# End of a feed-forward part: the last two up pairs first, then three down blocks by token chunk, with the weight ring turned one slot per layer

## The chip, the core and the metric

The kernel runs on one core of one Trainium2 chip. The metric is the device time of one execution in microseconds (us). Five engines work side by side, each through its own list in order: PE (TensorE, matmuls; PEld is its weight load), DVE (VectorE), ACT (ScalarE), POOL (GpSimd, which here only starts transfers) and SP (SyncE, which starts the weight transfers). They meet in semaphores.

## The reference

A trunk of two layers over 256 tokens of width 1024. Each layer has a mixer half and a feed-forward half, both between RMSNorms, with shift, scale and gate vectors computed from `c`:

```python
for l in range(DEPTH):                       # DEPTH = 2
    mod = c_act @ ada_w[l] + ada_b[l]
    sh_m, sc_m, g_m, sh_f, sc_f, g_f = jnp.split(mod, 6, axis=-1)
    h = modulate(rmsnorm(x, mix_pre_g[l]), sh_m, sc_m)
    y = mixer_sublayer(h, ...)
    x = x + g_m[:, None, :] * rmsnorm(y, mix_post_g[l])
    h = modulate(rmsnorm(x, ffn_pre_g[l]), sh_f, sc_f)
    up = causal_dwconv(h @ w_up, conv_w, conv_b)      # width 3, D_FF = 2816
    u, g = up[..., :D_FF], up[..., D_FF:]
    y = (jax.nn.gelu(g) * u) @ w_down
    x = x + g_f[:, None, :] * rmsnorm(y, ffn_post_g[l])
```

## The kernel before

**Split products.** Every f32 weight block and every activation is split into a high part and a low part, and a product is three matmuls (`mm3`, L1597). A weight block of 128 x 2048 goes through four stations: SP loads it into a slot of `raw`; ACT writes `w_hi` (L548, L925); DVE writes `w_lo` as the difference (L1039, L1541); PE multiplies. `raw`, `w_hi` and `w_lo` are rings of 3 slots (`RING`). SP may load a slot again when DVE has split its block (`lo_ready`), ACT may write `w_hi` when PE has used the block (`blk_used`). `SLOT[j]` says which slot block j of a layer takes: blocks 0 to 39 (`NM` = 40) are the mixer's, 40 to 72 (`NB` = 73) the feed-forward part's.

**Feed-forward part.** 22 tiles of the hidden width are worked in 11 pairs (`PAIRS`). Pair i has a gate block g(i), a value block u(i) (both up projections, 48 matmuls of 256 columns each) and a down block d(i). PE runs g(i), u(i), then d(i-1), which is 12 matmuls of 512 columns for token chunk 0 and 12 for chunk 1 (`down_proj`, L2034); the sums stay in banks 0 to 3. After g(i) and after u(i) ACT and DVE take the convolution out of the bank (`conv`, L902 and L1514), and then split the blocks that come next; `hidden` (L1532), `hidden_hi` (L917) and `hidden_lo` (L1536) make the input of d(i). The last pair ends with d(9) and d(10), each chunk 0 and then chunk 1. `gate_rows` (L1626) turns the gate vector into a row, in two halves, before g(10) and after u(10).

**Tile sums.** The shift, scale and gate vectors of the next parts are computed on DVE: tile by tile of `ada_w`, 128 x 1024 each, multiplied by `c` and summed (`ada_sum`, L1032, `ffn_sum`, L1557). POOL loads the tiles into two buffers of `adw` (L500): the load of tile n waits for the sum of tile n-2. In layer 0 the feed-forward part has 24 sums, most of them two to a pair; the last of them complete shift and scale of layer 1. Layer 1 has none from pair 3 on.

**End of a part.** `half_end` on DVE (L1132) begins with shift and scale (L1081, L1084), which need all sums. Then come `gated` for the two halves of chunk 0 (L1117, each after ACT's square of it, L616), `residual` of chunk 0 (L1129), the split of the next layer's block 0, `gated` of the first half of chunk 1, and `inverse_rms` (L1074, L1076), whose `diag` PE waits for with `to_features` (L1618). Then PE runs four filler matmuls (`keep_going`, L1632), the first product of the next layer, and `to_features` of chunk 1. At the end of layer 1 only `gated`, `residual` and the output transfers are left.

Of the kernel before, what the change touches and what calls it, by code (L numbers as in the profile page):

```python
# [21 lines left out]
P = 128  # L22
# [10 lines left out]
RING = 3  # L33
# [86 lines left out]
def trunk_kernel(nc, A, consts, out):  # L120
# [70 lines left out]
    assert SLOT[-RING:] == SLOT[:RING] == list(range(RING))  # L191
# [3 lines left out]
    def previous(j):  # L195

        before = [b for b in range(j) if SLOT[b] == SLOT[j]]
        return before[-1] if before else max(b for b in range(NB) if SLOT[b] == SLOT[j]) - NB

    ctx = ExitStack()  # L200
    with ctx:
# [74 lines left out]
        raw_in = [sig(f"raw_in{s}", 16 * USES[s]) for s in range(RING)]  # L276
# [89 lines left out]
        def slot_in(j):  # L366

            return raw_in[SLOT[j]]
# [9 lines left out]
        def block_shape(t, j):  # L378

            _, k, cols = mixer_blocks[j]  # L380
            return t[:, SLOT[j], 0:k * cols].rearrange("p (k n) -> p k n", k=k)

        def kv_parts(t, j, packed):


            v = t[:, SLOT[j], :].bitcast(F32) if packed == "read" else t[:, SLOT[j], :]
# [6 lines left out]
        def uq_parts(t, j, packed):  # L393


            v = t[:, SLOT[j], 0:QK * 4 * DQK]
# [26 lines left out]
        def _(sp):  # L423
# [4 lines left out]
            for n in range(ADA0):  # L428
# [5 lines left out]
                if n == 7:  # L434
                    j, (src, k, cols) = 0, mixer_blocks[0]
                    sp.dma_start(block_shape(raw, j), src(0)).then_inc(slot_in(j).s, 16)
            for l in range(L):
                for j, (src, k, cols) in enumerate(mixer_blocks):
# [3 lines left out]
                    sp.wait_ge(lo_ready.s, lo_ready.at(l, RING + previous(j) + 1))  # L442
# [4 lines left out]
                    sp.dma_start(block_shape(raw, j), src(l)).then_inc(slot_in(j).s, 16)  # L447
# [13 lines left out]
                def load(j_wait, slot, kind, src):  # L461
                    sp.wait_ge(lo_ready.s, lo_ready.at(l, j_wait))
                    sp.sem_inc(sp_tick, 1)
                    sp.dma_start(ffn_shape(raw, slot, kind), src).then_inc(raw_in[slot].s, 16)


                load(NM + 1, SLOT[NM], "up", up(l, FF, BW))
                load(NM + 2, SLOT[NM + 1], "up", up(l, 0, BW))
                with sp.Fori(1, PAIRS) as i:
                    load(3 * i + NM, SLOT[NM + 2], "up", up(l, i * BW + FF, BW))  # L470
                    load(3 * i + NM + 1, SLOT[NM + 3], "up", up(l, i * BW, BW))
                    down = A["ffn_w_down"][bass.ds(l, 1)].rearrange("a (k p) n -> p (a k) n", p=P)
                    load(3 * i + NM + 2, SLOT[NM + 4], "down", down[:, bass.ds(2 * i - 2, 2), :])
                down = A["ffn_w_down"][bass.ds(l, 1)].rearrange("a (k p) n -> p (a k) n", p=P)
                load(NB, SLOT[NB - 1], "down", down[:, 2 * PAIRS - 2:2 * PAIRS, :])
# [39 lines left out]
        def _(act):  # L515
# [27 lines left out]

            def split_hi(l, j, dst, src):

                act.wait_ge(slot_in(j).s, slot_in(j).at(l, 16 * (NTH[j] + 1)))
                act.wait_ge(blk_used.s, blk_used.at(l, RING + previous(j) + 1))
                A_(dst, src, ACT.Copy).then_inc(hi_ready.s, 1)  # L548

            def split_block(l, j):  # L550
                if j == J[("c", 2)]:

                    r = block_shape(raw, j)
                    d = w_hi[:, SLOT[j], :].rearrange("p (k n) -> p k n", k=DK)
                    act.wait_ge(slot_in(j).s, slot_in(j).at(l, 16 * (NTH[j] + 1)))
                    act.wait_ge(blk_used.s, blk_used.at(l, RING + previous(j) + 1))
# [3 lines left out]
                elif j == J[("ukv", 0)]:  # L560
                    act.wait_ge(slot_in(j).s, slot_in(j).at(l, 16 * (NTH[j] + 1)))
                    act.wait_ge(blk_used.s, blk_used.at(l, RING + previous(j) + 1))
                    for d, r in zip(kv_parts(w_hi, j, True), kv_parts(raw, j, False)):
                        a = A_(d, r, ACT.Copy)
                    a.then_inc(hi_ready.s, 1)
                elif j in (J[("uq", 0)], J[("uq", 1)]):
                    act.wait_ge(slot_in(j).s, slot_in(j).at(l, 16 * (NTH[j] + 1)))
                    act.wait_ge(blk_used.s, blk_used.at(l, RING + previous(j) + 1))
                    for d, r in zip(uq_parts(w_hi, j, True), uq_parts(raw, j, False)):
                        a = A_(d, r, ACT.Copy)  # L570
                    a.then_inc(hi_ready.s, 1)
                elif j < NM:
                    split_hi(l, j, block_shape(w_hi, j), block_shape(raw, j))
                else:
                    split_hi(l, j, w_hi[:, SLOT[j], :], raw[:, SLOT[j], :])
# [113 lines left out]
            for l in range(L):  # L689
# [210 lines left out]
                def conv(n, part, i, first=False):  # L900

                    product_done(act, l, NM + part if first else i * 3 + (NM - 1 + part))  # L902
# [12 lines left out]
                def hidden_hi(i, half=0):  # L915
                    act.wait_ge(f_t.s, f_t.at(l, i + 1))
                    A_(flat2(oa_hi, half), flat2(tmp, 0), ACT.Copy).then_inc(f_hi.s, 1)  # L917

                def ffn_split(i, part):

                    slot = SLOT[NM + 2 + part]
                    j = i * 3 + (NM + 2 + part)
                    act.wait_ge(raw_in[slot].s, raw_in[slot].at(l, i * 16 + 16 * (NTH[NM + 2 + part] + 1)))
# [9 lines left out]
                with act.Fori(1, PAIRS - 1) as i:  # L933
# [8 lines left out]
                i = PAIRS - 1  # L942
                gate_rows(l, 1, 0, 6)
# [4 lines left out]
                hidden_hi(i, 1)  # L948
# [10 lines left out]
        def _(dve):  # L959
# [81 lines left out]
            def split_block(l, j):  # L1041
                if j == J[("c", 2)]:
                    r = block_shape(raw, j)
                    h = w_hi[:, SLOT[j], :].bitcast(F32).rearrange("p (k n) -> p k n", k=DK)
                    d = w_lo[:, SLOT[j], :].rearrange("p (k n) -> p k n", k=DK)
# [1073 lines left out]
```

## Time and profile before

| | us |
|---|---|
| median of 3 runs | 997.36 (997.17 to 997.51) |
| profiled execution, its own time | 995.64 |
| its span in the trace | 994.0 |
| granted PE clock, mean | 0.991 |

The span is what the trace covers; some 1.6 us of the execution's time lie around it. Durations below come from this one execution. The "idle before" of an instruction names what ended the idle time. Matmul records overlap, since they are pipelined: the step from one to the next is what a matmul costs PE.

### The profile page before, as it was taken

How to read it: one execution, taken by the hardware profiler on the slowest of the kernel's cores; microseconds unless marked ns; L12 is line 12 of the kernel's file. 1: busy time of each engine (PE TensorE's matmuls, PEld its weight loads, DVE VectorE, ACT ScalarE, POOL GpSimd, SP SyncE). 2: the span in 40 equal slices, each digit the busy share in tenths (PEclk: the TensorE clock that was granted, in tenths of full speed). 3: DMA queues.
4: the chain of work that ended last, by engine and by line, in shares of the span. 5: the costliest groups of instructions: out<-in, count | busy, mean ns of one | idle time of the engine just before them, and what ended most of it. 6: DMA issues, size and time to landing. Idle time of an engine off the chain costs nothing.

```text
span 994.0 us, 17872 instructions
## 1 busy us (share of the span) xinstructions
PE 959.8 (97%) x6976; PEld 897.2 (90%) x6976; DVE 717.7 (72%) x958; ACT 526.3 (53%) x701; POOL 43.6 (4%) x85
## 2 busy tenths in 40 slices
PE   6899999999998999999989999999999999999997
PEld 6799989999987999999969999899999799999996
DVE  4689766676667888787776966677667689676675
ACT  4346855455446654554574475643445656554544
POOL 0000000000000100000000000000000000000000
PEclk9799999999999999999999999999999999999999
DMA  9985755556572787777636864556646557555541
GB/s 356 374 258 177 247 161 165 192 191 213 173 265 73 270 301 247 241 246 239 241 115 192 276 211 156 157 175 224 228 137 225 185 193 273 187 183 181 180 156 43
DMA packets 134138, 206.35 MB, mean 208 GB/s; under 512 B 6336, under 2 KB 104384, under 8 KB 133952
## 3 DMA queue, kind: packets, MB, share of 16 engines
q1 hardware_dynamic: 122416, 162.07, 49.9%
q0 software_dynamic: 11520, 41.95, 11.5%
q10 hardware_dynamic: 144, 1.51, 0.4%
q8 instruction: 42, 0.69, 0.3%
q14 instruction: 16, 0.13, 0.0%
HBM read 204.46 MB, written 1.05 MB: 207 GB/s over the span
## 4 chain that ended last, share of the span: by engine, by line
PE 88%; DVE 4%; ACT 3%; DMA 2%; SPq 1%; issue 1%; DVEq 0%; ACTq 0%
PE banks L1602 78%; DMA raw<-in_w_in 2%; PE banks L1618 1%; DVE w_lo L1039 1%; SPq L449 1%; PE banks L1888 1%; PE banks L1891 1%; PE banks L1626 1%; PE banks L1732 1%; PE banks L1714 1%; DMA raw<-in_ada_rows 1%; ACT h L597 1%; ACT w_hi L548 1%; DVE x L1129 1%; PE banks L1662 1%
## 5 line engine op out<-in xcount | busy, mean ns | idle before, releaser
L1602 PE MATMUL banks<-h_lo,w_hi 128*128 128x256 f32 x1504 | 430.5, 286 | 3.4 <-DVE h_lo L1100 3.0
L1602 PE MATMUL banks<-h_hi,w_lo 128*128 128x256 f32 x1504 | 425.5, 283 | 0.0
L1602 PE MATMUL banks<-h_hi,w_hi 128*128 128x256 f32 x1504 | 425.5, 283 | 0.0
L1602 PEld LDWEIGHTS banks<-h_lo,w_hi 128*128 128x128 f32 x1504 | 288.4, 192 | 7.1 <-DVE h_lo L1100 3.8
L1602 PEld LDWEIGHTS banks<-h_hi,w_lo 128*128 128x128 f32 x1504 | 288.5, 192 | 2.2 <-issue 1.4
L1602 PEld LDWEIGHTS banks<-h_hi,w_hi 128*128 128x128 f32 x1504 | 288.4, 192 | 0.0
L1039 DVE TENSOR_TENSOR w_lo<-raw,w_hi 128x2048 fp32r<-128x2048 f32 x82 | 187.2, 2290 | 71.0 <-ACT w_hi L548 70.8
L548 ACT ACTIVATE w_hi<-raw 128x2048 fp32r<-128x2048 f32 x82 | 156.0, 1911 | 120.1 <-PE banks L1602 99.1
L1541 DVE TENSOR_TENSOR w_lo<-raw,w_hi 128x2048 fp32r<-128x2048 f32 x56 | 128.0, 2286 | 22.6 <-ACT w_hi L925 22.6
L925 ACT ACTIVATE w_hi<-raw 128x2048 fp32r<-128x2048 f32 x56 | 107.2, 1914 | 41.8 <-PE banks L1602 41.8
L1518 DVE SCALAR_TENSOR_TENSOR EF<-banks,par,EF 128x254 f32<-128x254 f32 (+1 forms) x176 | 76.7, 477 | 49.9 <-ACT EF L906 44.5
L906 ACT ACTIVATE EF<-banks,par 128x256 f32<-128x256 f32 x88 | 45.1, 563 | 104.0 <-PE banks L1602 104.0
L1602 PE MATMUL banks<-w_hi,oa_lo 128*128 128x512 f32 x208 | 81.3, 391 | 0.0
L1602 PE MATMUL banks<-w_lo,oa_hi 128*128 128x512 f32 x208 | 81.2, 390 | 0.0
L1602 PE MATMUL banks<-w_hi,oa_hi 128*128 128x512 f32 x208 | 80.9, 389 | 0.0
L500 POOL DMA_DIRECT2D adw<-in_ada_rows x80 | 42.4, 531 | 792.5 <-DVE adw L1032 600.5
L1032 DVE SCALAR_TENSOR_TENSOR adw<-adw,cbc 128x1024 f32<-128x1024 f32 x58 | 70.4, 1221 | 5.7 <-DMA adw<-in_ada_rows 4.4
L836 ACT ACTIVATE lat<-banks 128x512 f32<-128x512 f32 x24 | 14.2, 590 | 74.6 <-PE banks L1602 74.6
L1602 PEld LDWEIGHTS banks<-w_hi,oa_hi 128*128 128x128 f32 x208 | 39.1, 188 | 8.2
L1602 PEld LDWEIGHTS banks<-w_hi,oa_lo 128*128 128x128 f32 x208 | 39.1, 188 | 7.6
L1602 PEld LDWEIGHTS banks<-w_lo,oa_hi 128*128 128x128 f32 x208 | 39.1, 188 | 7.4
L1602 PE MATMUL banks<-oa_lo,w_hi 128*128 128x256 f32 x128 | 37.2, 290 | 1.6 <-DVE EF L1467 1.6
(280 smaller groups left out, 1238.9 us busy)
## 6 DMA issues: line engine op xcount, KB each, us to landing
raw<-in_w_in SPq DMA_DIRECT2D x52, 1024.0 KB, 6.1
raw<-in_ffn_w_up SPq DMA_DIRECT2D x44, 1024.0 KB, 5.1
adw<-in_ada_rows POOLq DMA_DIRECT2D x80, 512.0 KB, 4.7
raw<-in_ffn_w_down SPq DMA_DIRECT2D x22, 1024.0 KB, 4.9
raw<-in_w_out SPq DMA_DIRECT2D x8, 1024.0 KB, 7.7
raw<-in_ret_wo SPq DMA_DIRECT2D x4, 1024.0 KB, 5.0
raw<-in_lru_wo SPq DMA_DIRECT2D x4, 1024.0 KB, 7.2
raw<-in_mla_wo SPq DMA_DIRECT2D x4, 1024.0 KB, 6.9
```

Source lines behind the costliest of these rows:

```text
L449: sp.dma_start(pos_i, A["positions"][0, :].partition_broadcast(P)).then_inc(pos_in, 16)
L500: pool.dma_start(adw[:, slot, :], ada_v[:, bass.ds(n + ADA0, 1), :].rearrange("p a d -> p (a d)")).then_inc(adw_in[slot], 16)
L548: A_(dst, src, ACT.Copy).then_inc(hi_ready.s, 1)
L597: a = A_(h32[:, k, cs], PS[:, ACT_BANK[c][half], P * i:P * i + P], ACT.Identity, scale=hscale[:, k:k + 1], bias=mod[:, k:k + 1])
L836: A_(flat2(lat, m % 2), PS[:, gate_bank(m), :], ACT.Tanh, scale=0.5).then_inc(mg_th.s, 1)
L906: a = A_(EF[:, 2 * part + b, :], PS[:, 4 + part, T * b:T * b + T], ACT.Identity, scale=par[:, l, bass.ds(i * 2 + col["tap2"] + NFF * (1 - ...
L925: A_(w_hi[:, slot, :], raw[:, slot, :], ACT.Copy).then_inc(hi_ready.s, 1)
L1032: V.scalar_tensor_tensor(adw[:, n % 2, :], adw[:, n % 2, :], 1.0, cbc[:], ALU.mult, ALU.mult, accum_out=mraw[:, n % NT:n % NT + 1]).then_i ...
L1039: V.tensor_tensor(dst, whole, hi, ALU.subtract).then_inc(lo_ready.s, 1)
L1518: v = V.scalar_tensor_tensor(EF[:, 2 * part + b, d:T], PS[:, 4 + part, T * b:T * b + T - d], par[:, l, bass.ds(i * 2 + col[f"tap{tap}"] + ...
L1541: V.tensor_tensor(w_lo[:, slot, :], raw[:, slot, :], w_hi[:, slot, :].bitcast(F32), ALU.subtract).then_inc(lo_ready.s, 1)
L1602: ins = MM(ps, lhs, rhs, start=first and n == 0, stop=last and n == 2)
```

## The change

It has four parts.

1. PE's order at the end of each feed-forward part: g(9), u(9), first half of `gate_rows`, g(10), u(10), second half, then d(8), d(9) and d(10) as d(8) chunk 0, d(9) chunk 0, d(8) chunk 1, d(10) chunk 0, d(9) chunk 1, d(10) chunk 1. The first half of `gate_rows` now waits for the convolution of g(9).
2. SP, ACT and DVE handle the last blocks in the order g(9), u(9), g(10), u(10), d(8), d(9), d(10). The hidden tiles of pairs 8, 9 and 10 go to three places (`hidden_tile`), since three are alive at once.
3. The blocks d(8), d(9), d(10) stand in slots 1, 2, 0 of the ring, so each layer's slots are turned by one (`at_slot`); the loads count per slot (`landed`).
4. The last sums of layer 0 move: one and then two in pair 8, none in pair 9, and three in a row after the split of d(10) (`last_sums`), ahead of `half_end`.

The core of the diff (the rest puts `at_slot(l, j)` for `SLOT[j]`):

```diff
+    END = NB - 5
+    for j, like in ((END, 7), (END + 1, 6), (END + 2, 8), (END + 3, 7), (END + 4, 6)):
+        SLOT[j] = SLOT[NB - 3 - like]
+    def at_slot(l, j):
+        return (SLOT[j] + l) % RING
...
 SP
-                with sp.Fori(1, PAIRS) as i:
+                with sp.Fori(1, PAIRS - 2) as i:
...
+                for j, i in ((END - 2, PAIRS - 2), (END, PAIRS - 1)):
+                    load_last(j, "up", up(l, i * BW + FF, BW))
+                    load_last(j + 1, "up", up(l, i * BW, BW))
+                for d in range(3):
+                    i = PAIRS - 3 + d
+                    load_last(END + 2 + d, "down", down[:, 2 * i:2 * i + 2, :])
...
 ACT
+                i = PAIRS - 2
+                conv(i * 2, 0, i)
+                split_block(l, END)
+                gelu(i)
+                conv(i * 2 + 1, 1, i)
+                split_block(l, END + 1)
+                split_block(l, END + 2)
+                hidden_hi(i)
+                gate_rows(l, 1, 0, 6)
+                i = PAIRS - 1
+                conv(i * 2, 0, i)
+                split_block(l, END + 3)
+                gelu(i)
+                conv(i * 2 + 1, 1, i)
+                split_block(l, END + 4)
+                hidden_hi(i)
                 gate_rows(l, 1, 1, 6)
...
 DVE
+                i = PAIRS - 3
+                conv(i * 2, 0, i)
+                split_block(l, END - 2)
+                last_sums(-6, -5)
+                conv(i * 2 + 1, 1, i)
+                split_block(l, END - 1)
+                hidden(i)
+                hidden_lo(i)
+                last_sums(-5, -3)
+                i = PAIRS - 2
+                conv(i * 2, 0, i)
+                split_block(l, END)
+                conv(i * 2 + 1, 1, i)
+                split_block(l, END + 1)
+                hidden(i)
+                hidden_lo(i)
+                split_block(l, END + 2)
                 i = PAIRS - 1
                 conv(i * 2, 0, i)
-                ffn_split(i, 0)
-                if l + 1 < L:
-                    ada_sum(l, 2 * NT - 2)
+                split_block(l, END + 3)
                 conv(i * 2 + 1, 1, i)
                 hidden(i)
-                hidden_lo(i, 1)
-                if l + 1 < L:
-                    ada_sum(l, 2 * NT - 1)
+                hidden_lo(i)
+                split_block(l, END + 4)
+                last_sums(-3, 0)
                 half_end(l, 1, 0)
...
 PE
+                up_pair(PAIRS - 2)
                 i = PAIRS - 1
+                pe.wait_ge(up_c.s, up_c.at(l, i * 2 - 1))
                 gate_rows(l, 1, 0, 6)
-                up_pair(i)
+                up_proj(i * 2, 0, s_g, RING + END + 1)
+                pe.wait_ge(up_c.s, up_c.at(l, i * 2))
+                up_proj(i * 2 + 1, 1, s_u, RING + END + 2)
...
-                for c in range(TC):
-                    down_proj(i - 1, s_d, i * 3 + (RING + NM + 2), False, False, c)
-                for c in range(TC):
-                    down_proj(i, SLOT[NB - 1], RING + NB, False, True, c, 1)
+                last_down(0, 0)
+                last_down(1, 0)
+                last_down(0, 1)
+                last_down(2, 0)
+                last_down(1, 1)
+                last_down(2, 1)
```

The first place is DVE at the end of layer 0, from the end of the last pair to the start of `half_end` (`hidden` writes `tmp`, `hidden_lo` writes `oa_lo` or `ob_lo`, an `adw` row is a tile sum). Before:

```order
L1532 TENSOR_TENSOR tmp<-EF 128x512 [waits up_c,f_gl]
L1536 TENSOR_TENSOR oa_lo<-tmp,oa_hi 128x512 [waits f_hi]
L1032 SCALAR_TENSOR_TENSOR adw,mraw<-adw,cbc 128x1024 [waits adw_in1]
L1081 TENSOR_TENSOR mod<-mraw,par 128x16 [waits ada_red]
L1084 SCALAR_TENSOR_TENSOR hscale<-mod,par 128x8 [waits mod_evac]
L1117 TENSOR_TENSOR CD<-banks,grow 128x512 [waits p_ss,grow_ev] x2
```

And DVE at the same place of the changed kernel:

```order
L1578 TENSOR_TENSOR tmp<-EF 128x512 [waits up_c,f_gl]
L1583 TENSOR_TENSOR ob_lo<-tmp,ob_hi 128x512 [waits f_hi]
L1085 TENSOR_TENSOR w_lo<-raw,w_hi 128x2048 [waits hi_ready]
L1078 SCALAR_TENSOR_TENSOR adw,mraw<-adw,cbc 128x1024 [waits adw_in1]
L1078 SCALAR_TENSOR_TENSOR adw,mraw<-adw,cbc 128x1024 [waits adw_in0]
L1078 SCALAR_TENSOR_TENSOR adw,mraw<-adw,cbc 128x1024 [waits adw_in1]
L1127 TENSOR_TENSOR mod<-mraw,par 128x16 [waits ada_red]
L1130 SCALAR_TENSOR_TENSOR hscale<-mod,par 128x8 [waits mod_evac]
L1163 TENSOR_TENSOR CD<-banks,grow 128x512 [waits p_ss,grow_ev] x2
```

A split and two more sums stand between `hidden_lo` and shift and scale; the first and the third sum use the same buffer of `adw`.

The second place is PE at the end of the down products of layer 0, up to `to_features` (`oa` holds the hidden tiles of all pairs before, of pairs 8 and 9 after; `ob` those of pair 10 after). Before:

```order
L1602 MATMUL banks<-w_hi,oa_lo 128x512
L1602 MATMUL banks<-w_lo,oa_hi 128x512
L1602 MATMUL banks<-w_hi,oa_hi 128x512
L1618 MATMUL banks<-diag,x 128x128 [waits n_dg]
L1618 MATMUL banks<-diag,x 128x128 x7
L1632 MATMUL banks<-cst 128x256 x4
```

And PE of the changed kernel, where the last matmul of d(10) chunk 0 is followed by d(9) chunk 1:

```order
L1670 MATMUL banks<-w_lo,ob_hi 128x512
L1670 MATMUL banks<-w_hi,ob_hi 128x512
L1670 MATMUL banks<-w_hi,oa_lo 128x512
L1670 MATMUL banks<-w_lo,oa_hi 128x512
L1670 MATMUL banks<-w_hi,oa_hi 128x512
```

Behind the last product of chunk 0 now stand 24 matmuls of chunk 1 (d(9), then d(10)), where 12 stood before; `to_features` and the four fillers follow as they did.

## Rows read from the trace of the kernel before

**Rows 1.** page: busy us of an engine (share of span) xinstructions

```profile
PE 959.8 (97%) x6976; PEld 897.2 (90%) x6976; DVE 717.7 (72%) x958; ACT 526.3 (53%) x701; POOL 43.6 (4%) x85
```

**Rows 2.** waits of PE, whole span: total us, times, longest

```profile
PE banks L1618 <- DVE diag L1076: 7.5, 6, 3.6
...
PE banks L1602 <- DVE h_lo L1100: 5.5, 3, 2.5
...
PE banks L1602 <- DVE w_lo L1039: 0.4, 1, 0.4
```

**Rows 3.** timeline, PE, layer boundary: start, us, line, what, [idle before]

```profile
510.35 2.99 PE L1618 MATMUL banks<-diag,x 128*128 128x128 f32 x16 [3.57 <-DVE diag L1076]
...
515.43 0.59 PE L1602 MATMUL banks<-w_hi,h_lo 128*128 128x512 f32 x1
...
519.31 2.05 PE L1618 MATMUL banks<-diag,x 128*128 128x128 f32 x16 [0.79 <-DVE diag L1076]
```

**Rows 4.** chain of waits, end of layer 0: start, us, what

```profile
483.47 11.51 PE banks L1602 x96
...
494.99 0.89 PE banks L1626 x8
...
495.88 8.20 PE banks L1602 x36
```

**Rows 5.** timeline of DVE, end of layer 0

```profile
494.34 1.22 DVE L1032 SCALAR_TENSOR_TENSOR adw<-adw,cbc 128x1024 f32<-128x1024 f32 x1
...
499.97 1.22 DVE L1032 SCALAR_TENSOR_TENSOR adw<-adw,cbc 128x1024 f32<-128x1024 f32 x1
...
501.24 0.17 DVE L1081 TENSOR_TENSOR mod<-mraw,par 128x16 f32<-128x16 f32 x1
...
501.44 0.17 DVE L1084 SCALAR_TENSOR_TENSOR hscale<-mod,par 128x8 f32<-128x8 f32 x1
...
503.81 0.69 DVE L1117 TENSOR_TENSOR CD<-banks,grow 128x512 f32<-128x512 f32 x1 [2.20 <-ACT CD L616]
...
504.89 0.69 DVE L1117 TENSOR_TENSOR CD<-banks,grow 128x512 f32<-128x512 f32 x1 [0.39 <-ACT CD L616]
...
507.02 2.29 DVE L1039 TENSOR_TENSOR w_lo<-raw,w_hi 128x2048 fp32r<-128x2048 f32 x1
```

**Rows 6.** timeline, POOL; landing of that issue; landings 430 to 512

```profile
496.30 0.53 POOL L500 DMA_DIRECT2D adw<-in_ada_rows  x1 [6.43 <-DVE adw L1032]
...
DMA to landing us min/median/max: 4.7/4.7/4.7
...
DMA to landing us min/median/max: 3.8/4.0/4.8
```

**Rows 7.** POOL and DVE after paired tile loads; landings 806 to 813

```profile
325.40 0.53 POOL L500 DMA_DIRECT2D adw<-in_ada_rows  x1 [38.25 <-DVE adw L1032]
...
332.20 1.23 DVE L1032 SCALAR_TENSOR_TENSOR adw<-adw,cbc 128x1024 f32<-128x1024 f32 x1 [2.50 <-DMA adw<-in_ada_rows]
...
DMA to landing us min/median/max: 6.2/6.7/7.1
```

**Rows 8.** stretches: busy by engine, then granted PE clock, DMA share, GB/s

```profile
511.00:512.00 1.00, 1.00 (x8) 1.00 (x7) 1.00 (x2) 1.00 (x2) 0.00 (x0) 0.62 0.94 284
...
514.00:515.00 1.00, 1.00 (x5) 0.86 (x4) 0.71 (x2) 1.00 (x4) 0.00 (x0) 0.67 0.01 3
```

**Rows 9.** timeline of DVE and ACT, late pair of layer 0

```profile
474.59 2.28 DVE L1541 TENSOR_TENSOR w_lo<-raw,w_hi 128x2048 fp32r<-128x2048 f32 x1
...
480.27 2.28 DVE L1541 TENSOR_TENSOR w_lo<-raw,w_hi 128x2048 fp32r<-128x2048 f32 x1
...
477.30 1.03 ACT L906 ACTIVATE EF<-banks,par 128x256 f32<-128x256 f32 x2 [1.96 <-PE banks L1602]
```

**Rows 10.** end of layer 1: ACT timeline, then the chain of waits

```profile
988.98 0.20 ACT L616 ACTIVATION_READ_ACCUMULATOR AB<-banks 128x1 f32 x1
...
989.29 0.29 DVE AB L1117
```

More of the change, by code:

```diff
@@ L197, in previous @@
         before = [b for b in range(j) if SLOT[b] == SLOT[j]]
-        return before[-1] if before else max(b for b in range(NB) if SLOT[b] == SLOT[j]) - NB
+        return before[-1] if before else max(b for b in range(NB) if SLOT[b] == (SLOT[j] + 1) % RING) - NB
+    def at_slot(l, j):
+        return (SLOT[j] + l) % RING
     ctx = ExitStack()
@@ L273, in PC @@
             return par[:, l, col[name] + i:col[name] + i + n]
-        raw_in = [sig(f"raw_in{s}", 16 * USES[s]) for s in range(RING)]
+        raw_in = [sem(f"raw_in{s}") for s in range(RING)]
         hi_ready = sig("hi_ready", NB)
@@ L364, in h_step, with hidden_tile, slot_in, landed @@
             return 2 * half + c + 1 if l == 0 and n < 2 else 2 * n + half + 1
-        def slot_in(j):
-            return raw_in[SLOT[j]]
+        def hidden_tile(i):
+            hi, lo, n = (ob_hi, ob_lo, 0) if i is PAIRS - 1 else (oa_hi, oa_lo, 2) if i is PAIRS - 2 else (oa_hi, oa_lo, 0)
+            return [t[:, n:n + 2, :].rearrange("p a b -> p (a b)") for t in (hi, lo)]
+        def slot_in(l, j):
+            return raw_in[at_slot(l, j)]
+        def landed(l, j, more=0):
+            earlier = sum(USES[(at_slot(l, j) - l0) % RING] for l0 in range(l))
+            return slot_in(l, j), more + 16 * (earlier + NTH[j] + 1)
         def product_done(eng, l, j):
@@ L1808, in uq @@
                     ready(l, j)
-                    wh, wl = weights(j)
+                    wh, wl = weights(l, j)
                     sg = (g_ev, lg_ev)[i]
@@ L1835, in _ @@
                 ready(l, j)
-                wh, wl = (t[:, SLOT[j], :].rearrange("p (k two n) -> p k two n", k=KVK, two=2) for t in (w_hi, w_lo))
+                wh, wl = (t[:, at_slot(l, j), :].rearrange("p (k two n) -> p k two n", k=KVK, two=2) for t in (w_hi, w_lo))
                 def uk(i):
@@ L1998, in out_proj @@
                     hi, lo = (ob_hi, ob_lo) if i < 2 else (oa_hi, oa_lo)
-                    wh, wl = weights(J[("out", i)])
+                    wh, wl = weights(l, J[("out", i)])
                     cs = slice(P * c, P * c + P)
@@ L2032, in up_proj, with down_proj @@
                     ins.then_inc(blk_used.s, 1)
-                def down_proj(i, slot, j_done, first, last, c, pair_half=0):
+                def down_proj(i, slot, j_done, first, last, c):
                     if c == 0:
@@ L2055, in _ @@
                 pe.wait_ge(n_lo.s, n_lo.at(l, 8))
-                s_g, s_u, s_d = SLOT[NM + 2], SLOT[NM + 3], SLOT[NM + 4]
-                up_proj(0, 0, SLOT[NM], RING + NM + 1)
-                up_proj(1, 1, SLOT[NM + 1], RING + NM + 2)
+                s_g, s_u, s_d = (at_slot(l, NM + 2 + part) for part in range(3))
+                up_proj(0, 0, at_slot(l, NM), RING + NM + 1)
+                up_proj(1, 1, at_slot(l, NM + 1), RING + NM + 2)
                 def up_pair(i):
```

143 lines of the change are left out of this document (78 added, 65 removed).

## The prediction

> **What bounds the kernel now.** I read the page first: PE is busy 959.8 of 994.0 us [rows 1], so time is PE's matmuls plus its idle places. Reordering matmuls changes nothing by itself. The waits of PE come next [rows 2]. The largest group is `to_features` waiting for `diag`: 7.5 us in 6 waits, 3.6 the longest. Waits for `h_lo` make 5.5 us. For a split weight block (L1039) PE waited 0.4 us once, and for L1541, the split of the feed-forward pairs, no row exists: weights arrive in time throughout. The timeline shows where the 3.6 lies: at the boundary of the two layers PE idles 3.57 us and restarts at 510.35 [rows 3], so it had ended its down products at 506.78. The chain of waits agrees: 48 matmuls from 495.88 at 8.20 / 36 = 0.228 us each end at 506.8 [rows 4]. A chunk of a down block (12 matmuls) is 2.73 us, a block 5.47, an up product 11.51 / 2 = 5.76.
>
> **PE's new order.** The same matmuls run, so the down products still end at 506.78 if nothing stalls. The last up product ended at 494.99 [rows 4]; with three down blocks behind it instead of two it ends 5.47 earlier, at 489.52. The result of chunk 0 is whole two chunks before the end instead of one, 2.73 us earlier. That is the possible gain: the normalisation of chunk 0 gets 2.73 us more cover.
>
> **Do weights arrive in time?** Four up products now stand in a row, with less PE work to hide the splits. In a late pair of layer 0 the low part of g(i+1) is written from 474.59 to 476.87, and u(i) is finished by 477.30, where ACT begins its convolution [rows 9]. PE then runs half of `gate_rows`, 0.89 [rows 4], so g(10) has at least 0.9 to spare. The low part of u(i+1) ends at 482.55, 5.25 after 477.30, and is wanted 0.89 + 5.76 = 6.65 after: 1.4 to spare, 1.1 if the 0.3 is taken off by which ACT starts after the product's end. On DVE then follow, counted from the end of u(9), by estimates from these rows: the split of u(10) to 5.5; hidden and its low part to 7.2 (from the end of the last up product to the end of these steps it is 494.99 to 499.97 [rows 4, 5], 4.98, of which 3.3 go by before the convolution ends); the split of d(8) to 9.4 at 2.2 each (2.29 busy at 507.02, of which 0.09 overlaps the next instruction [rows 5]); the convolution of g(10), 1.8, to 11.2; the split of d(9) to 13.4. d(8) is wanted at 13.3 and d(9) at 16.0. The split of d(10) is below. `gate_rows` waits for the convolution of g(9), over by then. SP's loads of g(10), u(10), d(8) are queued in this order behind the splits of g(9) and u(9), and each has over 6 us before ACT wants it. I cost all this at nothing; if a cover is missed by one DVE split it costs up to 2.2 us in each layer.
>
> **The turned ring.** It changes addresses and counts, no work. Block 2 of the next layer is loaded 8 us after where it was counted from the last up product, still some 25 us ahead of its use. Nothing.
>
> **The moved sums, which decide.** In layer 0, counted in the trace's time shifted by 5.47: `hidden_lo` of the last pair ended at 499.97, where the last sum began [rows 5]; now it ends at 494.50. The split of d(10) takes 2.2 and ends at 496.70, while PE wants it at 506.78 - 3 x 2.73 = 498.6: fine. Then sum 45 starts at 496.70, sum 46 some 1.2 later. Sum 47 uses sum 45's buffer. POOL starts a load 1.96 us after the start of the sum that frees the buffer: sum 494.34, issue 496.30 [rows 5, 6]. So tile 47 is issued at 498.66. It has to land before DVE can go on, and behind it are queued shift and scale, `gated`, `residual` and so `diag`: everything that the 2.73 us were for. Before, no sum waited there.
>
> How long does the landing take? The issue at 496.30, two microseconds behind the load of a weight block, took 4.7 us [rows 6]. The new one has the same block load ahead of it by the same distance, plus a second tile load (48, for layer 1) issued 1.2 us behind it. Bounds: below 3.8, the shortest of nine in this stretch [rows 6]; above 6.2 to 7.1, the two loads issued in a row at the end of layer 1's mixer half; the same pair in layer 0 has the issue at 325.40 and its sum at 332.20, 6.8 later, with DVE idle 2.50 for it [rows 7], there with two block loads in flight. I take 5.2: nearest to 4.7, half a microsecond for the companion.
>
> The Trainium skill has a rule on this: in "DMA: Bandwidth & Descriptors", section "Queues, rings and completion order", each transfer engine goes round between the queue rows packet by packet, and within one ring in order. By it the companion, in the same row, would take nothing from tile 47, and the landing would stay at 4.7, that is 0.5 us off the sum below. The rows do not settle it: the pair with 6.8 had more block loads beside it.
>
> The sum: tile 47 lands at 498.66 + 5.2 = 503.86. Sum 47 to shift is 1.27 (499.97 to 501.24), shift and scale 0.4 (501.24, 501.44, one more such step) [rows 5]: `gated` starts at 505.53. Before it started at 503.81, and PE restarted at 510.35, 6.54 later; 0.39 of these DVE waited for ACT's square [rows 5], which is long done now: 6.15, and 6.1 with DVE's closer spacing. PE restarts at 511.63, **1.3 us later than before**. At 4.7 it is 0.8, at 3.8 about 0, at 6.2 2.3, at 7.1 3.2. ACT's part of the chain (squares of x, block 1) shifts along.
>
> **The clock.** After the idle place the granted clock fell to 1.2 GHz at about 511.2 (0.62 of that microsecond) and rose at about 514.7 [rows 8], some 3.4 us, in which `to_features` and the fillers ran at half pace; the first product began at 515.43, 5.1 after the restart [rows 3]. With a longer gap the low stretch may start with the restart. If it ends where it did, PE has 0.4 us less work in it, a gain of 0.2; if it ends 4.3 us after the restart as before, 0.9 us more of it is at half pace, a loss of 0.5. I take 0.1 loss. The second wait for `diag`, 0.79 [rows 3], moves along.
>
> **End of layer 1.** No sums there. Chunk 0 is done earlier, but the last `gated` of chunk 1 starts at 989.29, right after ACT's square ended at 989.18 (988.98 + 0.20) [rows 10]: it hangs on the last matmul, not on chunk 0. Gain 0 to 0.1; I take 0.
>
> **Total.** 1.3 + 0.1 = 1.4. The profiled execution took 995.64 with a span of 994.0, so it would take 997.0. The median of the runs is 1.72 above it; on that basis 997.36 + 1.4 = **998.8**.
>
> **Rivals.**
> 1. *The landing is crowded.* Tile 47 lands after 6.2 to 7.1 us, as the pairs in [rows 7] did. For: two tile loads and a block load, 2 MB in all. Against: one block load, not two. Time: +2.3 to +3.2, with the clock up to +3.7: 999.7 to 1001.1. It decides from a landing of about 5.9.
> 2. *Chunk 0's cover counts in full.* If the third sum did not hold DVE, the restart would be 2.73 earlier, at 507.6, the gap 0.85, and the clock would have no reason to fall: 3.4 us at half pace would be saved, 1.7. Time: -2.7 to -4.4, 993.0 to 994.7. Against: the buffer is the same and its load needs 3.8 at least.
> 3. *No change.* Landing near 3.8 to 4.3: the two effects cancel, 997.2 to 997.9.
> 4. *Weights late.* The four up products outrun the splits, up to 2.2 in each layer on top: 1000 to 1003. Against: the spare 0.9 to 1.9 above.
>
> **How the numbers follow.** 0.2%, 2.0 us, is about what a measurement of this kernel can tell from no change. Forecast (landing 4.4 to 5.9) 0.53, rival 1 0.23, rival 2 0.07, rival 3 0.11, rival 4 0.06. The forecast and rival 3 lie within 2.0 us. So same 0.63, slower 0.30 (rivals 1 and 4 and a little of the forecast's upper edge), faster 0.07. The range leaves out rival 2 and the upper part of rival 4: 997.0 to 1001.0.
>
> **What would show it.** In the changed trace, DVE's third tile sum before shift and scale is preceded by 3 to 5 us idle, released by the transfer into `adw`; it starts before PE's last down matmul. PE's idle place at the boundary is 4.4 to 5.4 us. ACT's first square of chunk 0 comes over 5 us before the end of the down products, and DVE's `gated` stands far behind it. No PE wait for L1085 in the last pairs. The clock falls once there. I am wrong if DVE does not idle before the third sum, if PE waits between the up products, or if the gap is below 3.6.

## The result, and the profile after

| | before | after |
|---|---|---|
| median, us | 997.21 (995.59 to 1000.27, 20 runs) | 1000.05 (997.82 to 1000.94, 20 runs) |
| profiled execution, its own time | 995.64 | 999.12 |
| its span | 994.0 | 997.4 |
| granted PE clock, mean | 0.991 | 0.989 |

The ratio is 1.002, with a 95% interval from 1.0012 to 1.0028: the change makes the kernel some 2 us slower (1.2 to 2.8), about as much as a measurement can tell from no change. The two medians lie a little further apart, 2.84 us. In a second batch (11 runs, below) it was 1.0017 (1.0007 to 1.0027).

The page, then the waits of PE over the whole span (total us, times, longest), answer [rows 1, 2]:

```profile
PE 961.2 (96%) x6976; PEld 898.8 (90%) x6976; DVE 718.4 (72%) x958; ACT 525.2 (53%) x701; POOL 43.6 (4%) x85
```

```profile
PE banks L1686 <- DVE diag L1122: 9.0, 6, 4.5
PE banks L1670 <- DVE h_lo L1146: 5.7, 3, 2.8
...
PE banks L1670 <- DVE w_lo L1085: 0.3, 1, 0.3
```

The same number of matmuls ran. The wait for a split weight block is as small as it was, and the trace shows no wait of PE from 470 us to the end of the down products, so four up products in a row starved nobody. The wait for `diag` grew from 7.5 to 9.0. Where, the timeline of PE at the boundary of the layers shows, which answers [rows 3] (start, us, line, what, idle before):

```profile
511.79 3.59 PE L1686 MATMUL banks<-diag,x 128*128 128x128 f32 x16 [4.46 <-DVE diag L1122]
515.21 1.89 PE L1700 MATMUL banks<-cst 128*128 128x256 f32 x8
516.89 0.47 PE L1670 MATMUL banks<-w_hi,h_lo 128*128 128x512 f32 x1
...
521.22 2.05 PE L1686 MATMUL banks<-diag,x 128*128 128x128 f32 x16 [1.35 <-DVE diag L1122]
```

The gap is 4.46 where it was 3.57, and the second one 1.35 where it was 0.79. DVE's timeline says why, and answers [rows 5]:

```profile
494.45 0.69 DVE L1583 TENSOR_TENSOR ob_lo<-tmp,ob_hi 128x512 fp32r<-128x512 f32 x1 [0.70 <-ACT ob_hi L946]
495.06 2.28 DVE L1085 TENSOR_TENSOR w_lo<-raw,w_hi 128x2048 fp32r<-128x2048 f32 x1
497.26 1.22 DVE L1078 SCALAR_TENSOR_TENSOR adw<-adw,cbc 128x1024 f32<-128x1024 f32 x1
...
498.41 1.22 DVE L1078 SCALAR_TENSOR_TENSOR adw<-adw,cbc 128x1024 f32<-128x1024 f32 x1
...
504.17 1.23 DVE L1078 SCALAR_TENSOR_TENSOR adw<-adw,cbc 128x1024 f32<-128x1024 f32 x1 [4.54 <-DMA adw<-in_ada_rows]
...
505.74 1.28 DVE L1163 TENSOR_TENSOR CD<-banks,grow 128x512 f32<-128x512 f32 x2
```

The third sum waits 4.54 us for its tile. The chain of waits (start, us, what) runs through the same place, and on to PE:

```profile
498.71 0.49 issue
499.22 4.93 DMA adw<-in_ada_rows
504.17 1.25 DVE adw L1078 x2
...
511.44 0.30 DVE diag L1122
511.74 0.04 issue
511.79 0.58 PE banks L1686
```

ACT had both squares of chunk 0 before the tile had landed, and then stood idle (its timeline):

```profile
501.08 0.57 ACT L645 ACTIVATE CD<-banks 128x512 f32<-128x512 f32 x1
...
501.98 0.58 ACT L645 ACTIVATE CD<-banks 128x512 f32<-128x512 f32 x1
...
507.91 0.63 ACT L612 ACTIVATE lat<-x 128x512 f32<-128x512 f32 x1 [4.93 <-DVE x L1175]
```

So the new order did hand chunk 0 over early, and the hand-over lay unused for more than 3 us.

**Where the 3.4 us between the spans lie.** I cut each span at two places that need no clock: E, the end of layer 0's down products (the start of the first `to_features` less its gap), and the start of the second `to_features`. The middle stretch holds all that the change was expected to move.

| profile | E | E to second `to_features` | rest of the span |
|---|---|---|---|
| before | 506.78 | 12.53 | 474.7 |
| after | 507.33 | 13.89 | 476.2 |

The 3.4 are +0.55 at the start, +1.36 in the middle, +1.5 in the rest. Of the first, 0.4 is the first load of constants (4.4 us of waiting, 4.0 before); the other 0.15 was not traced. The last is no part of the change's work. It is a fall of the granted clock near 600 us, in the middle of products that PE never stopped. The stretches are of the changed kernel, then of the kernel before (busy by engine, clock, DMA share, GB/s):

```profile
600.00:602.00 2.00, 2.00 (x13) 2.00 (x13) 1.64 (x1) 1.97 (x4) 0.00 (x0) 0.60 0.00 0
602.00:604.00 2.00, 2.00 (x12) 2.00 (x12) 2.00 (x5) 0.05 (x1) 0.00 (x0) 0.55 0.12 8
```

```profile
600.00:602.00 2.00, 2.00 (x19) 2.00 (x19) 2.00 (x5) 0.15 (x1) 0.00 (x0) 1.00 0.23 16
602.00:604.00 2.00, 2.00 (x19) 1.88 (x19) 1.09 (x1) 0.88 (x1) 0.53 (x1) 1.00 0.73 285
```

PE reads as fully busy in all four rows, but started 25 matmuls where it had started 38: 13 x 0.105 (2.00 / 19) = 1.4 us. The experiments below show such falls in other kernels too, so the change itself is to be read from the middle stretch.

### The profile page after: what moved, and what is told of

It reads as the page before. It is cut to its first block, busy times and chain, and to the rows that moved or that the text cites. A ratio compares the mean times of both kernels' runs of the same rounds, so it can differ in the third digit from the quotient of the medians.

```text
span 997.4 us, 17698 instructions
## 1 busy us (share of the span) xinstructions
PE 961.2 (96%) x6976; PEld 898.8 (90%) x6976; DVE 718.4 (72%) x958; ACT 525.2 (53%) x701; POOL 43.6 (4%) x85
## 3 DMA queue, kind: packets, MB, share of 16 engines
q0 software_dynamic: 11520, 41.95, 11.6%
## 4 chain that ended last, share of the span: by engine, by line
PE 88%; DVE 4%; DMA 3%; ACT 2%; SPq 1%; issue 1%; DVEq 0%; POOLq 0%; ACTq 0%
PE banks L1670 78%; DMA raw<-in_w_in 2%; PE banks L1686 1%; DVE w_lo L1085 1%; SPq L467 1%; PE banks L1956 1%; PE banks L1959 1%; DMA raw<-in_ada_rows 1%; PE banks L1800 1%; PE banks L1782 1%; PE banks L1694 1%; ACT h L626 1%; PE banks L1966 1%; PE banks L1730 1%; PE banks L1819 1%
## 5 line engine op out<-in xcount | busy, mean ns | idle before, releaser
L1078 DVE SCALAR_TENSOR_TENSOR adw<-adw,cbc 128x1024 f32<-128x1024 f32 x62 | 75.0, 1219 | 10.5 <-DMA adw<-in_ada_rows 9.3
L1670 PE MATMUL banks<-w_hi,oa_lo 128*128 128x512 f32 x192 | 75.1, 391 | 0.0
L1670 PE MATMUL banks<-w_lo,oa_hi 128*128 128x512 f32 x192 | 74.9, 390 | 0.0
L1670 PE MATMUL banks<-w_hi,oa_hi 128*128 128x512 f32 x192 | 74.7, 389 | 0.0
L1670 PEld LDWEIGHTS banks<-w_hi,oa_hi 128*128 128x128 f32 x192 | 36.1, 188 | 7.7
L1670 PEld LDWEIGHTS banks<-w_hi,oa_lo 128*128 128x128 f32 x192 | 36.1, 188 | 7.0
L1670 PEld LDWEIGHTS banks<-w_lo,oa_hi 128*128 128x128 f32 x192 | 36.1, 188 | 6.8
```

The lines of the kernel that those rows point to most:

```text
L1078: V.scalar_tensor_tensor(adw[:, n % 2, :], adw[:, n % 2, :], 1.0, cbc[:], ALU.mult, ALU.mult, accum_out=mraw[:, n % NT:n % NT + 1]).then_i ...
L1670: ins = MM(ps, lhs, rhs, start=first and n == 0, stop=last and n == 2)
```

## The experiments

**1. One sum out of the row.** The theory: the third sum in a row holds DVE, and all that the order by chunk gives is behind it. In the changed kernel one sum goes back to pair 9.

```diff
                 split_block(l, END)
+                last_sums(-3, -2)
                 conv(i * 2 + 1, 1, i)
...
                 split_block(l, END + 4)
-                last_sums(-3, 0)
+                last_sums(-2, 0)
                 half_end(l, 1, 0)
```

> The changed kernel with one edit: sum 45 moves from the end of pair 10 to pair 9, behind the split of g(10), so two tile sums stand before shift and scale and neither uses a buffer freed just before. Theory A (the landing of tile 47 holds DVE and gives the loss): no idle before the last sum, PE's idle place at the layer boundary about 1.0 us instead of 4.46, no fall of the granted clock there, and 4 to 5 us less than the changed kernel, 2.7 to 3.5 less than the kernel before. Theory B (the loss comes from the new order of blocks or the turned ring): boundary gap stays above 3.5 us and the time within 0.1% of the changed kernel.

Measured: 995.66 (994.52 to 998.1, 12 runs), ratio 0.9984 (0.9973 to 0.9995), that is 1.8 us less than before where 2.7 to 3.5 were expected. DVE's idle time before the sums is gone, and it waits for ACT's square instead, 1.80. PE at the boundary:

```profile
507.99 2.05 PE L1687 MATMUL banks<-diag,x 128*128 128x128 f32 x16 [0.89 <-DVE diag L1122]
...
512.36 0.47 PE L1671 MATMUL banks<-w_hi,h_lo 128*128 128x512 f32 x1 [0.60 <-DVE h_lo L1146]
...
517.19 2.77 PE L1687 MATMUL banks<-diag,x 128*128 128x128 f32 x16 [1.82 <-DVE diag L1122]
```

The gap falls to 0.89, by 2.68 against before: chunk 0's cover counts almost in full (2.73). PE then gives part of it back, 0.60 for `h_lo` and 1.82 for the second `diag`, and the clock, which did not fall after the first gap, fell after the second, at 518 (2.77 for a `to_features` of 2.05). From the restart to the second `to_features` it is 9.20 (517.19 - 507.99), against 8.96 before, although the clock stayed up in this stretch. So the middle stretch fell by 2.44 (table below), and the fall of the clock at 518 lies behind it. That the waits and this fall are why the runs gained 1.8 and not 2.7 is argued from one profile.

**2. The three sums late in the kernel before.** The same cause, without the new order: the last three sums in a row after the last `hidden_lo`.

```diff
-                with dve.Fori(3, PAIRS - 1) as i:
+                with dve.Fori(3, PAIRS - 2) as i:
...
                 if l + 1 < L:
-                    ada_sum(l, 2 * NT - 2)
+                    ada_sum(l, 2 * NT - 4)
...
                 if l + 1 < L:
+                    ada_sum(l, 2 * NT - 3)
+                    ada_sum(l, 2 * NT - 2)
                     ada_sum(l, 2 * NT - 1)
```

> The kernel before with one edit: its last three tile sums of layer 0 stand in a row behind hidden_lo of the last pair, as the change has them; order of blocks and ring as before. Theory A: DVE idles about 4.5 us before the third, which starts 6.9 us after the first (first at 499.97, so 506.9), gated at 508.5, PE restarts about 4.3 us later than in the kernel before (gap near 7.9 us): 3.9 to 5.0 us slower than before. Theory B: the moved sums are hidden, within 0.5 us of before.

Measured: 1000.74 (999.11 to 1002.3, 10 runs), ratio 1.0032 (1.0021 to 1.0043). The row of sums alone, without any cover from a new order, costs 3.2 to 3.3 us. POOL's load of the third tile with its landing, then DVE, then PE:

```profile
503.64 0.53 POOL L500 DMA_DIRECT2D adw<-in_ada_rows  x1 [22.76 <-DVE adw L1032]
DMA to landing us min/median/max: 3.8/3.8/3.8
```

```profile
507.42 1.22 DVE L1032 SCALAR_TENSOR_TENSOR adw<-adw,cbc 128x1024 f32<-128x1024 f32 x1 [3.36 <-DMA adw<-in_ada_rows]
```

```profile
515.03 3.66 PE L1628 MATMUL banks<-diag,x 128*128 128x128 f32 x16 [6.53 <-DVE diag L1076]
```

The size was over-guessed: the gap is 6.53 where 7.9 was expected, and DVE waited 3.36 where 4.5 was expected. The tile landed after 3.8, not after the 4.9 of the changed kernel. The second load was again issued 1.15 behind it (504.79), but no weight block was in flight beside the two. So the companion cost the tile ahead of it nothing here.

**3. The down blocks back to block by block.** In the changed kernel, each block's two chunks one after the other again.

```diff
                 last_down(0, 0)
-                last_down(1, 0)
                 last_down(0, 1)
-                last_down(2, 0)
+                last_down(1, 0)
                 last_down(1, 1)
+                last_down(2, 0)
                 last_down(2, 1)
```

> The changed kernel with one edit: the three down blocks run block by block (each chunk 0, then chunk 1), not by chunk. Chunk 0 is whole 2.73 us later. Theory A: since DVE is held by the third sum until 505.7 anyway, chunk 0 (then whole at about 504.6) is still in time: the boundary gap stays 4.4 to 4.7 us and the time within 0.3 us of the changed kernel. Theory B (the order by chunk itself costs): 1 us or more faster than the changed kernel.

Measured: 998.49 (995.97 to 999.94, 12 runs), ratio 1.0008 (0.9998 to 1.0018). Within 0.3 of the changed kernel was expected; it came out 1.6 under it, in another batch, and so I ran both again together.

> The changed kernel once more, as the yardstick of this batch. Expected: 2.0 us slower than the kernel before (1.0012 to 1.0028 was measured), boundary gap 4.4 to 4.6 us, DVE idle 4.5 us before the third sum in a row. If the profiled run shows a fall of the granted clock near 600 us again it comes in most runs; each such fall is worth about 1.5 us and moves the whole run by a step.

> e3_by_block once more, beside the changed kernel on the same chip. Theory A: within 0.3 us of the changed kernel. Theory B (the order by chunk costs in itself): 1 us or more faster again, as the earlier ratios against the kernel before (1.0008 for it, 1.002 for the changed kernel) would have it.

Measured: the changed kernel 999.52 (997.72 to 1000.45, 11 runs), by block 998.96 (997.97 to 1000.09, 11 runs), ratios 1.0017 (1.0007 to 1.0027) and 1.0012 (1.0003 to 1.0021). The medians are now 0.56 apart and the intervals overlap. The profiles settle it better. The gap of the changed kernel, then of the one by block:

```profile
512.76 3.68 PE L1686 MATMUL banks<-diag,x 128*128 128x128 f32 x16 [4.44 <-DVE diag L1122]
```

```profile
512.41 3.67 PE L1686 MATMUL banks<-diag,x 128*128 128x128 f32 x16 [4.33 <-DVE diag L1122]
```

With the row of three sums in place the order of the down products makes no difference beyond a few tenths: DVE is held by the tile and not by chunk 0.

**4. Both: one sum out of the row, and block by block.** This asks what the order by chunk is worth once DVE is free; the edits are those of 1 and 3.

> Both edits: sums spread as in e1_spread, down blocks block by block as in e3_by_block. Theory A: the gap at the boundary is that of the kernel before, 3.4 to 3.7 us, the time that of the kernel before within 0.5 us, and 2.7 to 4.4 us slower than e1_spread: what the order by chunk is worth when DVE is free. Theory B: like e1_spread.

Measured: 997.1 (995.33 to 999.69, 12 runs), ratio 1.0 (0.9989 to 1.0011).

```profile
504.85 0.69 DVE L1163 TENSOR_TENSOR CD<-banks,grow 128x512 f32<-128x512 f32 x1 [4.02 <-ACT CD L645]
```

```profile
511.67 3.58 PE L1687 MATMUL banks<-diag,x 128*128 128x128 f32 x16 [3.57 <-DVE diag L1122]
```

The gap is that of the kernel before, 3.57, and DVE waits 4.02 for ACT's square, which waits for chunk 0. Against experiment 1 (0.89) the order by chunk takes 2.68 from the gap. Counted from the changed kernel by block (gap 4.33 and 4.53), the order by chunk alone takes nothing from the gap (4.44 and 4.46), the sum alone 0.8 to 1.0 (3.57), and both together 3.5 (0.89): a series of two waits of which the later one counts.

**5. Fillers in the gap.** What does the low clock after the gap cost? In the changed kernel, nine filler matmuls ahead of `to_features` (a filler matmul has two records, so the trace counts 18).

```diff
                 if l + 1 < L:
+                    keep_going(7, 9)
                     to_features(l + 1, 0, 0)
```

> The changed kernel with nine more filler matmuls of PE in the idle place, ahead of to_features (4.1 us of work in 4.46 us idle). Theory C (the low clock after the gap is a part of the loss): no granted clock below 1.0 between 508 and 518, to_features takes 2.0 us instead of 3.6, the first product of layer 1 starts 0.4 to 1.0 us earlier, and the time falls by 1.0 to 1.7 us against the changed kernel. If the clock hides behind the chain on DVE and ACT, the time falls by less than 0.4 us.

Measured: 999.74 (997.54 to 1001.26, 12 runs), ratio 1.0019 (1.0008 to 1.0031), as the changed kernel. PE:

```profile
508.43 4.05 PE L1700 MATMUL banks<-cst 128*128 128x256 f32 x18
513.02 2.05 PE L1686 MATMUL banks<-diag,x 128*128 128x128 f32 x16 [0.54 <-DVE diag L1122]
514.91 1.89 PE L1700 MATMUL banks<-cst 128*128 128x256 f32 x8
517.32 0.47 PE L1670 MATMUL banks<-w_hi,h_lo 128*128 128x512 f32 x1 [0.52 <-DVE h_lo L1146]
...
522.14 2.05 PE L1686 MATMUL banks<-diag,x 128*128 128x128 f32 x16 [1.82 <-DVE diag L1122]
```

The clock did not fall, `to_features` took 2.05 and not 3.59, and yet the second `to_features` came only 0.3 us sooner after the restart (522.14 - 513.02 = 9.12, against 521.22 - 511.79 = 9.43). Most of the 1.5 that PE saved turned into waits for `h_lo` (0.52) and for the second `diag` (1.82, 1.35 without fillers). After the restart DVE and ACT set the pace.

**6. The two diag steps earlier.** If DVE sets the pace, then what stands ahead of `diag` in its list does. On top of experiment 1, at this boundary only, the first `inverse_rms` goes ahead of one `gated`, and the second ahead of the split of block 1.

```diff
                 if ph == 1:
                     split_block(l2, 0)
+                if ph == 1:
+                    inverse_rms(l2, n2, 0)
                 gated(l, ph, 1, 0)
-                inverse_rms(l2, n2, 0)
+                if ph == 0:
+                    inverse_rms(l2, n2, 0)
...
                 if ph == 1:
-                    split_block(l2, 1)
                     inverse_rms(l2, n2 + 1, 1)
+                    split_block(l2, 1)
```

> e1_spread with DVE's inverse_rms moved at this boundary: for chunk 0 ahead of gated of chunk 1, for chunk 1 ahead of the split of block 1. In e1_spread PE still idled 0.89 us and 1.82 us for diag, and 0.60 for h_lo, and the clock fell at 518.8. Theory: the 1.82 goes (the split costs 2.2 of DVE ahead of it), the 0.89 falls to 0.3 to 0.9, the clock stays at 1.0 from 500 to 530, 2 to 4 us less than e1_spread. Rival: the chain of ACT (squares, modulation) ends last and the gaps move to h_lo: less than 1 us.

> The kernel with the sum of tile 45 spread and both diag steps ahead of the DVE work behind them, unchanged, in five more rounds. In its one profile the granted clock fell nowhere before the tail, and its 5 runs lay at 991.65 to 992.99. Theory A (its gain over the kernel with the spread sums alone, 3.6, is in part the two waits of PE at the boundary, about 0.6 and 1.8, and in part luck with the falls of the clock at start-up, near 115 and near 600, which every kernel here has in some runs): some runs come out 1.5 or 3 us higher, 993.5 to 995, and the profile may show a fall again near 116 or 600; the boundary itself keeps its form (gap 0.3, no wait of PE for the second diag). Theory B (the early diag removes those falls as well, since it keeps PE in step): all runs stay at 991.5 to 993.

Measured: 992.02 (991.65 to 992.99, 5 runs), ratio 0.9942 (0.9929 to 0.9954), and again 993.26 (991.64 to 995.87, 9 runs), ratio 0.996 (0.9948 to 0.9972). It beats both kernels, by 4 to 6 us against before.

```profile
507.23 2.05 PE L1690 MATMUL banks<-diag,x 128*128 128x128 f32 x16 [0.29 <-DVE diag L1122]
...
512.21 0.47 PE L1674 MATMUL banks<-w_hi,h_lo 128*128 128x512 f32 x1 [1.20 <-DVE h_lo L1146]
...
515.18 2.05 PE L1690 MATMUL banks<-diag,x 128*128 128x128 f32 x16
```

The last row has no idle time ahead of it. Of what PE gained there, part went into a longer wait for `h_lo`, 1.20 where it was 0.60. In the second batch the profile has the same form of the boundary (0.29 and 1.20 again), and runs came out up to 4 us higher, so part of the 992.0 was luck, most likely with the clock elsewhere. The rival, that the early steps keep all runs at 991.5 to 993, did not hold (five of nine took 993.3 to 995.9); but both profiles are of runs under 992, so that falls near 116 or 600 made the slower ones is not shown.

**7. The diag steps alone, on both kernels.** The same edit on the changed kernel, and on the kernel before.

> The changed kernel, with the three sums in a row left as they are, and only the two diag steps put ahead of one gated row and of one weight split on DVE. Theory A (both steps stand on the path from the third sum to PE): the first gap falls by about 0.6, from 4.5 to 3.9, the second, 1.35, goes, together some 2 us: 997.5 to 998. Rival (the second diag is not on the path, since PE then waits for h_lo or for a weight block instead): 0.6 only, 999.1 to 999.4. If the falls of the clock elsewhere depend on these steps, more than 3: under 996.5.

> The kernel before, with only the two diag steps put ahead. PE waited 3.57 and 0.79 there. Theory A: 2.9 and nothing, 1.3 to 1.5 less: 995.8 to 996.1 against 997.3. Then the spread sums with the order by chunk (992.0) keep some 3 to 4 us over this kernel, and what the changed kernel gives away is its row of three sums. Rival (the two diag steps alone make most of the gain of the 992.0 kernel, and the new order at the end little): 994 or less.

Measured: 996.89 (995.15 to 999.21, 11 runs), ratio 0.9998 (0.9988 to 1.0009), and 996.46 (994.71 to 997.64, 11 runs), ratio 0.9993 (0.9983 to 1.0003). The gaps are 3.94 and 2.97, the second gap is gone in both. By the medians the steps give 2.6 on the changed kernel (2.0 expected, and its 999.52 is of another batch) and about 1 on the kernel before (1.3 to 1.5 expected); by the middle stretches of the table below they give 2.1 and 1.5, as expected. So these steps alone do not explain the 992 to 993. That kernel needs all three: chunk 0 early, DVE not held by a tile, `diag` ahead of what PE does not wait for. With all three the middle stretch is 8.24; without the early `diag` it is 10.09 (experiment 1), without the spread sum 11.80, and without the new order, in the kernel before with the early `diag`, 11.00.

**8. The kernel before once more,** for the falls of the clock.

> The kernel before, unchanged, profiled once more. All profiles so far split into three stretches: up to the end of the down products of layer 0 (506.6 to 507.3 without a fall of the clock near 116, 508.1 to 508.5 with one), from there to the second to_features (12.53 in the kernel before, 13.89 in the changed one), and the rest (474.7 to 475.0 without a fall near 600, 476.1 to 476.4 with one). Theory (the falls near 116 and 600 come by execution and not by the change): the middle stretch is 12.5 again, 12.4 to 12.7; the first and the last take one of their two values each, so the span is 994.0, 995.4 or 996.8 within 0.4, and the records show the falls that go with it. Rival (the falls belong to the changed kernels): no fall at 116 and 600, span 993.6 to 994.4, and the runs that take longer have another cause.

Measured: 997.32 (995.7 to 1001.65, 9 runs); span 994.4, no fall near 116 or 600, middle stretch 12.75, a little over the 12.4 to 12.7 expected (`to_features` lay in the low clock for 3.49 instead of 2.99). That is what the rival had said of this run, no fall and a span of 993.6 to 994.4; the theory allowed it as one of its three values. So this run does not decide between them, and two profiles of the kernel before now show no such fall. Against a tie to the new order stand the two variants of the kernel before in the table, which have no new order and show both falls. All profiles, cut as above (with fillers, E is where these start):

| profile | E | E to second `to_features` | rest | clock falls near 116, near 600 |
|---|---|---|---|---|
| before | 506.78 | 12.53 | 474.7 | no, no |
| before, again | 506.98 | 12.75 | 474.7 | no, no |
| before, diag early | 508.37 | 11.00 | 476.2 | yes, yes |
| before, three sums late | 508.50 | 15.87 | 476.2 | yes, yes |
| changed | 507.33 | 13.89 | 476.2 | no, yes |
| changed, again | 508.32 | 13.96 | 476.1 | yes, yes |
| changed, by block | 506.67 | 14.16 | 476.1 | no, yes |
| changed, by block, again | 508.08 | 13.85 | 476.1 | yes, yes |
| changed, filled | 508.43 | 13.71 | 476.4 | yes, yes |
| changed, diag early | 508.23 | 11.80 | 475.0 | yes, no |
| one sum out | 507.10 | 10.09 | 477.7 | no, yes |
| one sum out, by block | 508.10 | 13.00 | 476.1 | yes, yes |
| one sum out, diag early | 506.94 | 8.24 | 475.0 | no, no |
| the same, again | 506.63 | 8.23 | 475.0 | no, no |

Three things can be read off. The first and the last column take two values each, about 506.9 or 508.3 and 474.9 or 476.2 in the mean, and the value goes with the fall (477.7 holds the fall at 518 besides). The same kernel, profiled twice, shows both kinds at 116: 507.33 and 508.32. And the middle stretch repeats within 0.1 for two of the four kernels profiled twice and within 0.2 to 0.3 for the other two, so it tells what an edit does better than a median of twelve runs: changed +1.4, three sums late in the kernel before +3.3, one sum out -2.4, that with the diag steps early -4.3.

## Why the prediction was right, step by step

- **Same work, weights in time, the ring free of cost.** Right. The up products of the last pairs ran without a wait. The spare at u(10) was costed at 1.1 to 1.4; nothing there was ever late.
- **The row of three sums decides.** Right, and by the mechanism named. Counted back from E (506.78 before, 507.33 after), the first sum was to start at -10.08 and started at -10.07 (497.26); the issue of tile 47 was to come at -8.12 and came at -8.11 (499.22); the third sum was to start at -2.92 and started at -3.16 (504.17). From the issue to the sum it is 4.95 us, where I had taken 5.2: the landing took 4.9, 0.2 over the 4.7 of [rows 6] and not 0.5. Whether the 0.2 is the companion's is not shown: in experiment 2 the tile landed after 3.8 with a companion behind it, as one alone. The crowded 6.2 to 7.1 of [rows 7] did not come. The Trainium skill ("DMA: Bandwidth & Descriptors", section "Queues, rings and completion order") says that each ring is worked in order and that a transfer engine goes round between the rows; by this the companion takes nothing from the tile ahead. The 3.8 of experiment 2 agrees with it, and the 4.9 here lies between it and my half microsecond.
- **From there to PE.** `gated` followed the third sum in 1.57, not 1.67, and PE restarted 6.05 after it (6.1 taken). The gap was to grow by 1.3 and grew by 0.89.
- **The clock and the second wait for diag.** This term was mis-sized. I took 0.1 for the clock and let the second gap of 0.79 move along. At PE's first product the clock did cost nothing: it started 5.10 after the restart, as before (5.08). But `to_features` ran at 1.2 GHz over nearly its whole length (3.59, before 2.99), as the stretches that answer [rows 8] show:

```profile
512.00:513.00 1.00, 1.00 (x5) 1.00 (x6) 0.96 (x3) 1.00 (x1) 0.00 (x0) 0.50 0.90 180
...
515.00:516.00 1.00, 1.00 (x7) 0.92 (x7) 0.58 (x2) 1.00 (x3) 0.00 (x0) 0.98 0.33 107
```

  The chain of waits before led from `residual` straight to the first `modulate` on DVE (L1093); now it leads through `to_features` (L1139 is the same `modulate`). Before, then after:

```profile
511.00 0.70 DVE x L1129
...
512.33 0.73 DVE h L1093 x2
```

```profile
511.79 2.09 PE banks L1686 x8
...
513.97 0.74 DVE h L1139 x2
```

  So the first `modulate` began 2.18 after the restart and not 1.98, ACT's last `h_hi` 5.42 and not 4.97, and the second `to_features` 9.43 and not 8.96. These 0.47 are this term, the upper bound of the -0.2 to +0.5 that the prediction gave; experiment 5, without the slow clock, gets 0.3 of them back. With 0.89 + 0.47 = 1.36 the middle stretch is what the sum said, 1.4, but from two terms that were each off by 0.4, in opposite directions. That they cancelled was luck.
- **The end of layer 1.** Right: nothing. Its last `gated` in the chain comes 3.38 later than in [rows 10], which is what the start, the boundary and the fall near 600 had put there (0.55 + 1.36 + 1.5). The reading behind the term was too simple, though: in the chain before, that `gated` followed DVE's work on chunk 0, from 988.02 to 989.23, and ACT's square of chunk 1 ended at 989.18, so both ways ended within 0.1. Handing chunk 0 over early removed only the first. The chains, before and then after:

```profile
988.02 0.74 DVE x L1129
```

```profile
975.50 16.36 PE banks L1670 x72
...
992.67 0.29 DVE AB L1163
```

- **The total** was 998.8 on a base of 997.36; the medians were 1000.05 and 999.52, that is 2.84 and 2.15 over those of before in the same batches. Of this the middle stretch accounts for 1.4. The remaining 0.8 to 1.4 is in no term of the prediction. It would fit one fall of the clock more in the typical run (12 of the 20 runs of the changed kernel in the first batch took 999.7 or more), but a run without a profile has only its mean clock on record, not where it fell, and the mean does not sort the runs: runs of the kernel before at 997.4 to 997.5 have 0.984, 0.988 and 0.996. Whether the change makes these falls more frequent, or the batches only drew them so, is not settled. Both profiles of the kernel before show none near 116 or 600, and its runs still lie at about 996, 997.4 and 999.
- **The rivals.** That chunk 0's cover counts in full (-2.7 to -4.4) was wrong for this change, but right in mechanism: with one sum taken out of the row the gap fell by 2.68. Its second part, 1.7 for the clock, was wrong: in experiment 1 the clock stayed up after the gap and the way to the second `to_features` was no shorter (9.20 against 8.96), and experiment 5 gives 0.3.

## What to carry to other kernels

Before work is moved to the end of a stretch, look at what feeds it: a sum that was free in the middle cost DVE 4.5 us of idle time here once it was third in a row on two buffers, and everything behind it waited. An earlier hand-over is worth only what the next engine in the series can take up at once. Here one edit that took nothing from the gap alone and one that took 0.9 took 3.5 together, and then moving two steps ahead of work that PE did not wait for gave another 1.8. To compare variants that lie 1 us apart, cut their profiles at the same events around the edit before trusting medians.

## What the runs showed of the hardware

- **The granted clock can fall while PE shows no idle time** near it, at the same places of the program in many kernels (near 116 and near 600 us), in one profile of a kernel and not in the next. The one near 600 of the changed kernel is 3.4 us at 1.2 GHz: the two stretches of 2 us lack 0.40 and 0.45 of the full clock, and at half the clock that is (0.40 + 0.45) x 2 x 2. Over all profiles such a fall made its stretch 1.3 to 1.4 us longer. That would fit the runs of the kernel before, which lie at about 996, 997.4 and 999. What sets the falls off was not found.
- **Falls near the start cost nothing that can be seen.** The kernel with one sum out and `diag` early showed no fall until the last 2 us in its first profile; in its second the clock was low from 11.6 to 15.0 and from 21.9 to 35.6 us, and the span was 989.9 against 990.2.
- **A low clock after a gap can be free.** `to_features` at half pace took 1.5 us longer and moved the next meeting of the engines by 0.3, since DVE and ACT had as much to do.
- **A tile load of 512 KB landed in 4.9 and 5.0 us** when two were issued 1.15 apart beside one weight block, against 3.8 for one issued alone at 506.14 and 6.2 to 7.1 at the end of the mixer half [rows 7]. With a second load 1.15 behind and no weight block beside, it was 3.8 too, and 4.4 for the second (experiment 2).
